# A hybrid decoder trunk: eight tile pairs a layer as block products, three of them in a row in two groups

## The reference

```python
h = rmsnorm(x, p["ffn_norm"][layer])
up = h @ p["w_up"][layer]                      # 1024 -> 2 * 2816
c, fb = causal_dwconv(up, ffn_bufs[layer], p["ffn_conv_w"][layer], p["ffn_conv_b"][layer])   # 3 taps
x = x + (jax.nn.silu(c[..., :D_FF]) * c[..., D_FF:]) @ p["w_down"][layer]
new_ffn.append(fb)
```

## Time and profile before

| | us |
|---|---|
| three runs, median | 1164.09 (1163.95 to 1164.12) |
| the profiled execution | 1163.62 |
| its span, first to last instruction | 1161.9 |
| TensorE busy | 1145.3 (99%), 8442 matmuls |
| VectorE / ScalarE / GpSimd busy | 818.0 (70%) / 580.0 (50%) / 722.1 (62%) |
| granted TensorE clock | 0.998 of full |

### The profile page before, as it was taken

One profiled execution on the slowest core, in us unless ns is written; L12 is line 12 of the kernel. 1 busy time (PEld: TensorE's weight loads), 2 busy tenths in 40 slices (PEclk: granted clock), 3 DMA queues, 4 the chain that ended last, 5 costly groups with the idle time before them and its releaser, 6 DMA issues. The chain is left out here.

```text
span 1161.9 us, 21843 instructions
## 1 busy us (share of the span) xinstructions
PE 1145.3 (99%) x8442; PEld 1124.9 (97%) x8442; DVE 818.0 (70%) x1506; ACT 580.0 (50%) x1113; POOL 722.1 (62%) x691
## 2 busy tenths in 40 slices
PE   8999999999999999999999999999999999999997
PEld 8887999999999999999999999999999999999997
DVE  5999768878677867775614644388686778678655
ACT  7475555544554555453613533366346545654543
POOL 3996344359867985872564324334698679768633
PEclk9999999999999999999999999999999999999999
DMA  6311242203421422131422222322042213232312
GB/s 233 117 56 36 67 146 81 93 28 95 142 65 44 149 73 92 56 137 51 149 84 91 69 69 74 117 82 65 28 147 91 80 61 116 74 92 80 120 51 82
DMA packets 35688, 104.01 MB, mean 90 GB/s; under 512 B 5105, under 2 KB 7153, under 8 KB 35569
## 3 DMA queue, kind: packets, MB, share of 16 engines
q1 hardware_dynamic: 31504, 98.92, 26.9%
q10 hardware_dynamic: 4080, 3.69, 1.1%
HBM read 98.29 MB, written 4.79 MB: 89 GB/s over the span
## 5 line engine op out<-in xcount | busy, mean ns | idle before, releaser
L594 PE MATMUL psum<-x_hi,w_hi 128*128 128x320 f32 (+2 forms) x1564 | 336.4, 297 | 1.3 <-POOL w_lo L1664 1.3
L594 PE MATMUL psum<-x_lo,w_hi 128*128 128x320 f32 (+2 forms) x1564 | 334.8, 295 | 0.0
L594 PE MATMUL psum<-x_hi,w_lo 128*128 128x320 f32 (+2 forms) x1564 | 334.1, 295 | 0.0
L1664 POOL TENSOR_TENSOR w_lo<-w_raw,w_hi 128x1024 fp32r<-128x1024 f32 (+1 forms) x84 | 181.8, 2169 | 188.0 <-ACT w_hi L1041 188.0
L594 PEld LDWEIGHTS psum<-x_hi,w_hi 128*128 128x128 f32 x1564 | 258.8, 188 | 3.6 <-POOL w_lo L1664 1.6
L594 PEld LDWEIGHTS psum<-x_hi,w_lo 128*128 128x128 f32 x1564 | 258.5, 188 | 0.0
L594 PEld LDWEIGHTS psum<-x_lo,w_hi 128*128 128x128 f32 x1564 | 257.3, 188 | 0.0
L2412 DVE SCALAR_TENSOR_TENSOR psum<-arena,params,psum 128x608 f32<-128x608 f32 x176 | 150.4, 854 | 58.8 <-ACT psum L1420 55.8
L1806 POOL TENSOR_TENSOR w_lo<-arena,w_hi 128x384 fp32r<-128x384 f32 x120 | 130.8, 1109 | 49.6 <-ACT w_hi L1331 49.6
L839 PE MATMUL psum<-block_hi,w_lo 128*128 128x288 f32 x504 | 149.2, 296 | 0.0
L839 PE MATMUL psum<-block_hi,w_hi 128*128 128x288 f32 x504 | 149.2, 296 | 0.0
(11 more groups left out here) (270 smaller groups left out, 2207.1 us busy)
## 6 DMA issues: line engine op xcount, KB each, us to landing
w_raw<-in_w_up SPq DMA_DIRECT2D x44, 512.0 KB, 3.7
arena<-in_w_up SPq DMA_DIRECT2D x44, 512.0 KB, 4.3
arena<-in_w_down SPq DMA_DIRECT2D x24, 384.0 KB, 3.6
w_raw<-in_w_down SPq DMA_DIRECT2D x24, 384.0 KB, 3.2
w_raw<-in_w_in_c SPq DMA_DIRECT2D x16, 512.0 KB, 3.5
w_raw<-in_w_in_ab SPq DMA_DIRECT2D x11, 512.0 KB, 3.6
w_raw<-in_w_out_ab SPq DMA_DIRECT2D x16, 256.0 KB, 2.7
w_raw<-in_w_out_c SPq DMA_DIRECT2D x8, 512.0 KB, 3.6
```

The costliest lines, as they stand in the source:

```text
L594: last = nc.tensor.matmul(PS[:, 2 * (q % 2 if slot is None else slot) + half, 0:b - a], w[q][:, k * P:(k + 1) * P], r[:, r_at, a:b], start ...
L1664: nc.gpsimd.tensor_tensor(w_lo[slot][:, 0:nk * P], raws[RAW_SLOT[RAW[u]]][:, 0:nk * P], w_hi[slot][:, 0:nk * P].bitcast(F32), ALU.subtract ...
```

## The change

```diff
-    PATTERN = ("PPPPPP", "PPSPSP", "PPSPSP", "PPPP")
+    PATTERN = ("PPPPPS", "PPSSSP", "PPSSSP", "PPSP")
...
                         for n in range(1, 7):
                             if n in (1, 2, 3, 5):
                                 bank_copy(layer, g, i, PAIR_ORDER[n - 1])
+                            if n == 1 and after_s(g, i):
+                                silu(i - 1)
                             weights_hi(layer, g, AHEAD[g][(h, i), n])
...
                         tap0(i, 0, u + 3)
-                        silu(i)
                         tap0(i, 1, u + 8)
+                        if not following_s(g, (h, i)):
+                            silu(i)
...
-                        pad(t, 0)
-                        pad(t, 1)
                         for n in range(7):
                             weights_lo(layer, g, AHEAD[g][(h, i), n])
+                            if n == 4:
+                                pad(t, 0)
+                                pad(t, 1)
```

## The result

| | before | after |
|---|---|---|
| median, us | 1164.02 (1163.89 to 1164.12, 4 runs) | 1176.55 (1175.73 to 1177.34, 4 runs) |
| profiled execution / its span | 1163.62 / 1161.9 | 1175.73 / 1174.0 |
| matmuls / TensorE busy | 8442 / 1145.3 | 8346 / 1138.2 |
| GpSimd busy | 722.1 (62%) | 788.2 (67%) |

The ratio is 1.0108 (1.0096 to 1.012): the changed kernel is 12.5 us slower, where I had forecast 7. It is half a microsecond above the top of my range. Note that its runs lie 1.6 us apart, those of the kernel before 0.2.

The account below looks back on a forecast made before the run. TensorE, busy 1145.3 of 1161.9 us, was taken as the bound. Groups 1 and 2 +9.8, group 0 +0.1, group 3 -2.8 gave +7.0 on 1163.62: 1170.6, plus 0.47 to the median, forecast 1171.1; range 1162.5 to 1176.0.

Parts of the forecast that it names:

- TensorE's saving, 11.7 us: Four plain pairs a layer become block pairs: 4 x 1.50 + 4 x 1.42 = 11.7 us less TensorE work.
- Waits in the groups of three, 3.94: Groups 1 and 2: late GpSimd state copies make TensorE wait twice, 3.94 us; less 1.50 saved, each group 2.44 longer.
- The chain's t: Zero point of the prediction's times: TensorE's start on the first block pair of a group, 881.17 in its rows.
- From the tap to TensorE's start, 2.62: ScalarE's two taps, high half of product 5 and copy of A11, plus two semaphores, ahead of TensorE's product S2: 2.62 us.
- Group 0, no wait counted inside its block pair: Group 0's block pair: GpSimd's light load is done near t+10.0, ahead of the tap, so no wait was counted.
- Group 0, third down product: Behind group 0's block pair: TensorE waits 1.45 us for the third down product, against a gain of 1.42; two layers +0.1.
- Group 3, -2.8: Group 3's one block pair, with a plain pair behind it, has no wait: 2 x -1.42 = -2.8 us.
- rival (c): The granted clock falls in TensorE's gaps, 2 us lost once in each group of three, adding 8: 1179; chance 0.05.
- The interference: VectorE's own weight sum slows a GpSimd operation beside it by 0.46 us; the skill page's rule would allow 0.77.
- The moved SiLU: With SiLU behind both first taps, VectorE's chain after a block pair ends about 1.5 us earlier, with no gain for TensorE.

Follow-up runs that it names:

- outer_blocks_sooner: Kernel before plus the changed groups 0 and 3 only, with ScalarE making the hidden blocks ahead of the fourth high half at group 0's end: 1159.38 us.
- short_vector_sum: threes alone, with VectorE's own weight sum behind a block pair made for only 8 of its 512 columns: 1171.81 us.
- sums_on_vector: threes alone, with VectorE instead of GpSimd making all three weight sums of a block pair that follows a block pair: 1173.92 us.
- eight_pairs_mended: Changed kernel with sums S1 and S2 on VectorE, state copies ahead of R3, hidden blocks sooner and A11 copied earlier in the outer groups: 1155.87 us.
- order_only: Kernel before's pattern of block pairs, with the changed kernel's new order of SiLU and state copies: 1163.89 us.
- threes alone: Changed kernel with three block pairs in a row in groups 1 and 2 and none in groups 0 and 3 (also threes_only): 1177.78 us.
- all_together: Changed kernel with all three following-pair sums on VectorE, hidden blocks sooner at group 0's end, and A11 copied earlier behind a plain pair: 1171.63 us.
- twos_only: Changed kernel with two block pairs side by side in groups 1 and 2, none in groups 0 and 3: 1171.12 us.
- copies_first: threes alone, with GpSimd's state copies back ahead of its first low half, as in the kernel before: 1175.56 us.
- silu_between: threes alone, with ScalarE's SiLU back between the two first taps of a block pair: 1198.5 us.
- s1_on_vector: threes alone, with state copies ahead of the sums and, behind a block pair, sum S1 on VectorE, R3 then S2 on GpSimd: 1166.17 us.

## Why the prediction was right or wrong, point by point

The direction and the main mechanism were right: GpSimd, with 13.7 us of work for 11.24 of TensorE, makes TensorE wait twice in each group of three. The size was not: 12.5 us slower, not 7. The step that failed outright is group 0, whose block pair was given no wait of its own. The waits of the groups of three were sized too low, and the fall of the clock was left out of the sum.

- **TensorE's saving, 11.7 us:** right. 96 matmuls fewer, and a block pair without waits takes 11.24.
- **Waits in the groups of three, 3.94:** the mechanism, its place and its period (13.73) were right; the waits were 4.15, and a group came out 2.83 longer, not 2.44: 4 x 0.39 = 1.6 us too low. The first wait was put at 1.45 and is 1.79. The chain's t of the earlier trace rows is 0.16 later than the first matmul's start, so TensorE wants the copy that much sooner; the pause between the sums was 0.22 and not 0.17; and from the start of the state copies to the tap it is 0.29 (318.93, 319.22), where the sum had 0.20. The second wait was 2.36 and not 2.49. The 0.08 behind each wait was in no row before. All of these are small, but they stood in one serial chain that TensorE waits for, in four groups.
- **From the tap to TensorE's start, 2.62:** measured 335.59 - 332.95 = 2.64. Right.
- **Group 0, no wait counted inside its block pair:** this step failed, 2 x (0.60 + 0.08). I looked at GpSimd's load only and took ScalarE's and VectorE's rows of group 1 for it. Both block pairs come behind a plain pair; what differs is the hidden block of that plain pair. The kernel makes it in a short form for the first three pairs of a group and in a long one, with more sums on VectorE, for the last three. In group 1 it is that of pair 0, in group 0 that of pair 3. By the two timelines VectorE is still at it when TensorE ends the tile, the weight sum comes next, and the tap starts at t+1.94 and not t+1.12 (from the first matmul's start).
- **Group 0, third down product:** 1.65 instead of 1.45, of which 0.16 is again the chain's t; with the 0.08 behind it, twice 0.3. Right in kind, and outer_blocks_sooner took it away.
- **Group 3, -2.8:** right. No wait there.
- **The clock, rival (c):** I priced it at 2 us for each group and gave it 0.05. It happened in one group of four in the profiled run, for 1.5 us. Taken as all or nothing it was unlikely; as a part of the forecast's own range it was missing, and with 1.5 us for one group the range would have held the result.
- **The interference:** the row's 0.46 a sum was right for GpSimd (short_vector_sum: 0.45). The page "SBUF — State Buffer" of the Trainium skill, section "Who interferes with whom", has the loser fully blocked for the whole instruction; on GpSimd's side the trace does not show 0.77. On VectorE's side the prediction allowed for up to 0.6 a sum, which had slack in this change. A sum takes 0.68 us where GpSimd is idle (233.47 above), 1.50 in sums_on_vector, and 4.42 in one place of eight_pairs_mended; it was the sums_on_vector mend that paid for that.
- **The moved SiLU:** "for nothing" was said of the plain pair behind, and order_only agrees. For block pairs in a row it is worth 21 us, falls of the clock included.

So of the 5.4 us between forecast and result, 1.6 are the groups of three, 1.9 group 0 (+2.0 against +0.1), 1.5 the clock in the profiled run and 0.1 the rest. The last 0.35 are the step from profiled execution to median: 0.82 here, the profiled run being the shortest of the four, where I had added 0.47. (The terms of the prediction's sum give 6.98 and not 7.04, which leaves its 7.0 as it is.) Whether more falls of the clock make up that 0.82 is in no trace; the granted clock of the two longest runs (0.996 against 0.997) speaks for it.

## What to carry to other kernels

When a change makes two costly stages neighbours, work out the period of each engine over one stage and compare it with the bound: 13.7 us of GpSimd against 11.24 of TensorE said in advance that GpSimd would fall back. No order tried here hid that, and the first version with block pairs in a row to gain had taken work off GpSimd. Then follow the chain across engines behind each thing that was late, since the first mend (copies sooner) and the second (sums moved) each uncovered the next link. And read the rows of a stage at its own place: the missed wait stood where the pair ahead was of the same kind, but had the long form of the hidden block to make.

## What the runs showed of the hardware

- **TensorE's clock can fall after short gaps, and not every time.** Gaps are idle times here, in the profiled runs and away from the program's ends. The granted clock went to the lower level behind one of four gaps of 2.2 us in the changed kernel, one of four with threes alone, two of four of 1.96 us in all_together, none of four of the same length in sums_on_vector, one of four of 1.7 to 1.8 us in short_vector_sum, and the one of 2.35 us in eight_pairs_mended; behind none of 20 gaps of 1.6 us (changed kernel, threes_only, twos_only, all_together, copies_first). With longer gaps it fell in most cases: in silu_between at four of four of 4.1 us and three of four of 2.4 to 2.9 us (not at one of 2.69), and behind the one of 4.26 us in s1_on_vector. A fall after the short gaps cost 1.5 us. What decides between two gaps of one length stays open. The Trainium skill, page "TensorE: Matmul & The Clock Gate", section "Why this matters for your kernels", advises against idle gaps above a length that it gives; here gaps of 1.8 to 2.4 us, shorter than that, were sometimes enough.
- **A VectorE sum with both operands in SBUF can take six times as long beside GpSimd operations that stand in a row:** 4.42 and 4.47 us instead of 0.70 to 0.75, in two profiled runs, at places where it took the short time in the other groups. Both ended about 0.55 us after the last of GpSimd's operations, which went at full pace, so I read it as VectorE being shut out; no run takes GpSimd's operations away there. In other places a sum beside GpSimd's work cost GpSimd 0.45 us and VectorE 0 to 0.8.
